# Hybrid decoder block on one core: router weights loaded earlier, into a buffer of their own

## The reference

```python
h = rms_norm(x, g_mix_norm)
proj = h @ w_in                                  # 1024 x 7168: q, k, v, g_ret, u_pool, gate_a, gate_b
merged = sigmoid(gate_a) * (y_ret @ w_branch[0]) + sigmoid(gate_b) * (y_pool @ w_branch[1])
x = x + merged @ w_out
h2 = rms_norm(x, g_ffn_norm)
logits = h2 @ w_router + b_router                # 1024 x 32
top_val, top_idx = top_k(logits, 4); top_w = softmax(top_val)
# every expert e, for the tokens that chose it:
act = swiglu_clamped(h2 @ w_gate_up[e] + b_gate_up[e])     # 1024 x 2048
x += top_w * (act @ w_down[e] + b_down[e])                  # 1024 x 1024
x = x + sigmoid(rms_norm(x, g_ple_norm) @ w_ple_gate) * (p @ w_ple_proj)
y = rms_norm(x, g_final)
```

## Time and profile before

| | before |
|---|---|
| median of three executions | 1283.8 us |
| profiled execution, its time | 1294.33 us |
| profiled execution, its span | 1292.5 us |
| mean granted TensorE clock | 0.957 |
| PE busy | 1219.5 us, 94% |
| DVE, ACT, POOL busy | 383.1, 202.0, 8.3 us |
| bytes moved, share of q1 of the 16 DMA engines | 456.59 MB, 85.2% |
| chain that ended last | PE 74%, DMA 14%, DVE 9% |

### The profile page before, as it was taken

One profiled execution on the slowest core, in us unless ns is written; L12 is line 12 of the kernel. 1 busy time (PEld: TensorE's weight loads), 2 busy tenths in 40 slices (PEclk: granted clock), 3 DMA queues, 4 the chain that ended last, 5 costly groups with the idle time before them and its releaser, 6 DMA issues.

```text
span 1292.5 us, 13525 instructions
## 1 busy us (share of the span) xinstructions
PE 1219.5 (94%) x5404; PEld 612.8 (47%) x5405; DVE 383.1 (30%) x587; ACT 202.0 (16%) x266; POOL 8.3 (1%) x19
## 2 busy tenths in 40 slices
PE   7999999969999999999999899999999999899987
PEld 6888888834443434343434344334344343434335
DVE  6955666521221303030312212202212030303036
ACT  5354444320100000010100000000000000001024
POOL 0000000000000000000000000000000000000000
PEclk9999999979999999999999999899999999999998
DMA  9754355866899999999999999869999999999970
GB/s 363 265 177 163 119 203 188 323 243 277 327 404 423 430 426 417 425 425 421 426 414 417 430 412 427 352 283 426 427 415 428 418 430 407 407 418 429 428 281 33
DMA packets 56621, 456.59 MB, mean 353 GB/s; under 512 B 5406, under 2 KB 6860, under 8 KB 30316
## 3 DMA queue, kind: packets, MB, share of 16 engines
q1 hardware_dynamic: 54320, 451.99, 85.2%
q10 hardware_dynamic: 2268, 4.14, 0.9%
HBM read 455.07 MB, written 1.05 MB: 353 GB/s over the span
## 4 chain that ended last, share of the span: by engine, by line
PE 74%; DMA 14%; DVE 9%; issue 1%; ACT 1%; SPq 0%; DVEq 0%; POOLq 0%; POOL 0%; ACTq 0%
PE ps L559 74%; DMA ring<-in_w_gate_up 12%; DMA B<-in_b_router 2%; DVE B L1469 2%; DVE x L1480 2%; DVE B L1460 2%; DVE B L1465 2%; DVE B L1461 2%; PE ps L566 1%; SPq L475 0%; DMA x<-in_x 0%; DVE over_xn L1257 0%; ACT B L1128 0%; ACT over_hT L1010 0%; PE ps L825 0%
## 5 line engine op out<-in xcount | busy, mean ns | idle before, releaser
L559 PE MATMUL ps<-ring,B 128*64 128x512 f32 x3024 | 685.5, 613 | 14.2 <-DMA ring<-in_w_gate_up 12.7
L559 PEld LDWEIGHTS ps<-ring,B 128*64 128x64 f32 x3024 | 223.7, 141 | 463.6 <-issue 459.8
L1460 DVE TENSOR_SCALAR B<-ps 128x1024 f32<-128x1024 f32 x16 | 19.6, 1225 | 667.5 <-PE ps L559 667.5
L559 PE MATMUL ps<-w_split,over_hT 128*128 128x512 f32 x544 | 173.8, 396 | 2.9 <-DVE w_split L1248 2.7
L1248 DVE TENSOR_TENSOR w_split<-ring,w_split 128x1024 fp32r<-128x1024 f32 x88 | 105.9, 1223 | 72.2 <-ACT w_split L1002 70.3
L559 PEld LDWEIGHTS ps<-w_split,over_hT 128*128 128x128 f32 x544 | 103.0, 191 | 24.7 <-issue 3.1
L559 PE MATMUL ps<-w_split,over_xn 128*128 128x512 f32 x288 | 113.1, 393 | 0.0
L1002 ACT CAST w_split<-ring 128x1024 fp32r<-128x1024 f32 x88 | 91.2, 1054 | 105.3 <-PE ps L559 105.0
L1119 ACT ACTIVATE B<-B 128x1024 f32<-128x1024 f32 x16 | 16.9, 1056 | 570.4 <-DVE B L1460 570.4
L559 PE MATMUL ps<-B 128*128 128x512 f32 (+3 forms) x288 | 92.0, 493 | 1.9 <-ACT B L1128 1.2
L559 PE MATMUL ps<-B,xn 128*128 128x128 f32 x512 | 73.9, 311 | 13.3 <-DVE x L1480 13.3
(11 more groups left out here) (140 smaller groups left out, 384.4 us busy)
## 6 DMA issues: line engine op xcount, KB each, us to landing
ring<-in_w_gate_up SPq DMA_DIRECT2D x120, 2048.0 KB, 13.5
ring<-in_w_down SPq DMA_DIRECT2D x60, 2048.0 KB, 15.9
ring<-in_w_in SPq DMA_DIRECT2D x28, 1024.0 KB, 5.1
ring<-in_w_gate_up SPq DMA_DIRECT2D x12, 1024.0 KB, 9.7
ring<-in_w_branch SPq DMA_DIRECT2D x8, 1024.0 KB, 7.0
ring<-in_w_down SPq DMA_DIRECT2D x6, 1024.0 KB, 13.2
ring<-in_w_out SPq DMA_DIRECT2D x4, 1024.0 KB, 4.9
ring<-in_w_ple_gate SPq DMA_DIRECT2D x4, 1024.0 KB, 16.3
```

Source lines behind the costliest of these rows:

```text
L559: return pe.matmul(out, lhsT, rhs, start=start, stop=stop, skip_group_check=True)
L1460: step(ve.tensor_scalar(gate, two_banks(0), LIMIT, None, ALU.min), s.gate_ready)
```

## The change

Before, the router's weights and bias were pieces of `B[4]`, loaded when the last merge had been read. Now they have a tensor of their own, `router`, 288 numbers in each partition, and the two loads stand behind the four copies of the pooling's mix, ahead of the loads of `b_down` and `g_final`.

```diff
+        router, = sb("router", [P, (KD + 1) * N_EXPERTS])
...
-        w_router = piece(KD * N_EXPERTS).rearrange("p (k e) -> p k e", k=KD)
-        b_router = piece(N_EXPERTS)
+        w_router = router[:, 0:KD * N_EXPERTS].rearrange("p (k e) -> p k e", k=KD)
+        b_router = router[:, KD * N_EXPERTS:]
...
                 nc.scalar.copy(mixedT[:, 2 * j:2 * j + 2, :], bank_cols(4 + j, 2)).then_inc(mixT_ready, 1)
 
+            e.dma_start(w_router, t["w_router"][0].rearrange("(k p) n -> p k n", p=P)).then_inc(router_loaded, 16)
+            e.dma_start(b_router, t["b_router"].to_broadcast([P, N_EXPERTS])).then_inc(router_loaded, 16)
             e.dma_start(b_down, t["b_down"][0]).then_inc(late_loaded, 16)
             e.dma_start(g_final, t["g_final"].unsqueeze(0).to_broadcast([P, D])).then_inc(late_loaded, 16)
             read_block(11, gates[0], ACT.Sigmoid)
...
             e.wait_ge(branch_read, 4)
-            e.dma_start(w_router, t["w_router"][0].rearrange("(k p) n -> p k n", p=P)).then_inc(router_loaded, 16)
-            e.dma_start(b_router, t["b_router"].to_broadcast([P, N_EXPERTS])).then_inc(router_loaded, 16)
             e.dma_start(p_in, t["p"][0, 0].rearrange("(i p) n -> p i n", p=P)).then_inc(p_loaded, 16)
...
-    nc = bacc.Bacc("TRN2", target_bir_lowering=False, num_devices=1)
+    nc = bacc.Bacc("TRN2", target_bir_lowering=False, num_devices=1, dynamic_dma_scratch_size=1024)
```

## The result

| | before | changed |
|---|---|---|
| median, first comparison | 1283.8 us (5 runs) | 1274.95 us (5 runs) |
| ratio, 95% interval | | 0.9914, 0.9894 to 0.9934 |
| second comparison, other runs | 1288.0 us | 1274.46 us, 0.9911 (0.9885 to 0.9936) |
| third | 1288.0 us | 1275.58 us, 0.9906 (0.9882 to 0.9929) |
| profiled execution, its time / span | 1294.33 / 1292.5 us | 1279.28 / 1277.4 us |

The ratio is an estimate of its own from the executions of both kernels, with its 95% interval; it is not the quotient of the two medians, and the two can differ by some us. By the ratios the change gains 0.9%, which is 11 us; by the medians of the first comparison it gains 8.9. The forecast was 1268.6 us, a gain of 15.2.

The account below looks back on a forecast made before the run. The prediction took PE's 9.86 us wait for the router's bias, with half-clock work behind it, as the bound ahead of nearly weight-bound experts. Gains of 12.2 + 2.6 + 0.4 = 15.2 us gave 1268.6 us, range 1264.5 to 1275.

Parts of the forecast that it names:

- The bound and the rigid shift: PE's 9.86 us wait for the router's bias; removing it moves first gate product and weight stream forward together by 15.2 us.
- Term 1: Last transposes to the end of the router's product: wait gone and product at full clock, 12.2 us gained.
- Term 2: From the router's product to the gather: bias products and ranks take 5.1 instead of 7.74 us, 2.6 us gained.
- Term 3: The gather ahead of the first pair: clock dips as in pair 2, 5.7 instead of 6.10 us, 0.4 us gained.
- clock stays up: Rival, from the router on: without the idle time the clock never falls, 16.9 us gained, 1266.9 us; chance 0.18.
- clock is lower for longer: Rival, router to gather: little-work products keep the clock down, 9.5 to 13 us gained, 1271 to 1274.3 us; chance 0.13.
- held at the new place: Rival: the queue takes small descriptors only as they move, holding ACT at about 155 us; slower, 1310 us; chance 0.04.
- swallowed by weights: Rival, experts' stage: PE, 15 us early, waits 15 us for weights; no gain, 1283.8 us; chance 0.05.

Follow-up runs that it names:

- place_only: Changed kernel with its own router tensor and smaller descriptor space, but the router's two loads issued at the old place: 1289.08 us, ratio 1.0019.
- after_fill: Changed kernel with 11 filling products of 128 x 512 on PE ahead of the router's product: 1284.29 us, ratio 0.9973.
- after_again: Changed kernel run again with no edit, against the kernel before: 1274.46 us, ratio 0.9911.
- before_again: Kernel before, unchanged, timed against itself: 1285.85 against 1288.0 us, ratio 0.9988.
- after_third: Changed kernel run once more with no edit, against the kernel before: 1275.58 us, ratio 0.9906.
- fill_wait: Kernel before, loads at the old place, with 11 filling products keeping PE busy during the router wait: 1283.82 us, ratio 0.9976.
- long_rows: Kernel before, loads at the old place, w_router read as 8 whole rows per partition, leaving token routing wrong: 1273.68 us, ratio 0.9869.
- bias_rows_first: Changed kernel with the first pair's bias products over 128 rows instead of 2: 1271.94 us, ratio 0.9861; repeated, 1272.96 us, 0.988.
- bias_rows_all: Changed kernel with the bias products of all 16 pairs over 128 rows instead of 2: 1271.37 us, ratio 0.9852.

## Why the prediction was right, and where its sizes were off

**The bound and the rigid shift: right.** PE waited 9.86 us for a load of 16 KB, and nothing but the time of its issue had to change (place_only). SP's first load behind `used` moved by the same 13.56 us as the first gate product, and 9.6 us of filling cost 8.0 to 9.8 (after_fill against after_again). In eight of the profiles the time from the first gate product to the end is

| loads late | us | loads early | us |
|---|---|---|---|
| before | 995.9 | changed kernel | 994.4 |
| before_again | 993.2 | after_again | 987.9 |
| place_only | 990.1 | after_third | 989.9 |
| fill_wait | 990.6 | after_fill | 990.5 |

The means are 992.5 and 990.7, so early loads don't make this stage longer, as far as eight profiles that scatter over 8 us can tell. The other four profiles lie in the same band: long_rows 989.9, bias_rows_first 989.7 and 994.1, bias_rows_all 992.2.

**Term 1, 12.2 us: right.** The product ended at 281.88 and now ends at 266.33 + 3.64 = 269.97; with the 0.29 us that this execution lags, 12.2. The start right behind the transposes, the 3.5 us (3.64) and DVE's scaling in time all came as worked out. The split into wait and clock is shown by fill_wait.

**Term 2, 2.6 us: measured 2.2.** From the router's end to the gather it is 5.51 us instead of 7.74. The ranks came 4.2 instead of 4.0 after the router's end, and the fourth bias bank ran partly at half clock.

**Term 3, +0.4 us: measured -0.6. This is the step that was mis-sized.** I took from pair 2 that the clock falls 4.8 us after the bias begins and is back 3.4 later. Here it fell after 3.9 and stayed down for about 6.8, so the gather took 6.67 instead of the forecast 5.7; the profiles of after_again, fill_wait, after_fill and long_rows have it down for 6.8 us too. The direction of the weighing was right: products over 2 rows, not idle time, bring the clock down before the gather, so the rival "clock stays up" fell, and bias_rows_first shows both halves of that. What failed is the reason for the size, "the same kind of work in the same order". More pairs would not have helped, since 19 of the 21 stretches at half clock that the kernel before has between 300 and 1250 us last the same 3.4 us. But in pair 2 the bias is followed by gate products over 512 columns, and here by the ranks, the fourth bank and a gather over 128. PE's timeline of the kernel before behind the bias of pair 2:

```profile
405.74 2.59 PE L559 MATMUL ps<-ring,B 128*64 128x512 f32 x8
```

The row for this very place stood in the earlier trace rows: before the change, the clock was down from 284.0 to 294.2, 10.2 us, through the same products. The 6.8 us lie between that and pair 2's 3.4. Why the dip is 6.8 us long stays open: no run varies what stands behind the bias products.

Together 12.2 + 2.2 - 0.6 = 13.8 us, and less the 0.3 lag the 13.56 by which the first gate product moved. It lies between the forecast's 15.2 and the up to 13 of the rival "clock is lower for longer". In its mechanism this rival was half right: the clock was low for twice as long as forecast, though it stayed at 1.00 through the router's product, from 266 to 274.

**From 13.8 to the measured 11.** The three ratios give 11.0, 11.5 and 12.1 us, the medians 8.9, 13.5 and 12.4. The experts' stage alone scatters over 8 us between the profiles above. The upper ends of the gains' intervals are 13.6, 14.8 and 15.2 us, so two of the three hold 13.8, and the first just misses it. The 8.9 owes most to the kernel before, whose median was 1283.8 in that comparison and 1288.0 in the two others, while the changed kernel's stayed within 1.1 us. So the 2.8 us between 13.8 and 11, twice as much as the 1.4 by which the terms were off, are in part scatter. What remains open is whether 1 to 2 us are lost systematically, behind the first gate product or by the new place; no profile shows where. The 15.1 us between the two first spans looked like a full hit and was none: 1.5 us of it is a shorter experts' stage.

**The other rivals.** ACT was not held at the new place: the loads were through in 4 us, and the four issues took ACT 2.87. The gain was not swallowed by weights: the first load behind `used` came at 286.73, where 285 was forecast, and no gate product of the first pair waited for a unit. The landing was far quicker than the 28 us I allowed for, which changed nothing.

## What to carry to other kernels

Here a small load, issued beside a saturated stream, landed late by its number of packets and not by its bytes. Two remedies are to issue it earlier or to give it long rows; either was worth about 1% here, though a version with long rows and the right routing was not run. When a wait of TensorE goes, count also what ran at half clock behind it, but look for other causes of a low clock in the same place before crediting it. How long such a stretch lasts is not safely taken from another place: it was 3.4 us in most pairs, 10.2 at this place before the change and 6.8 after it. Where the next stage is bound by transfers, ask whether those transfers are released by the engine that comes earlier: here they were, and the shift arrived at the end, in full or nearly so.

## What the runs showed of the hardware

- On this kernel, products with 2 of 128 rows are followed by half the TensorE clock although the engine is busy; the same products with 128 rows, 126 of them against zeros, keep it at 2.4 GHz ahead of the first pair (gather 6.62 to 6.78 us in three profiles of the changed kernel, 4.01 in three with 128 rows).
- `p`, behind the router's loads in ACT's queue, landed 29.9 us after issue before, 10.4 in the changed kernel, and 17.4 in long_rows, where fewer packets stood ahead of it: its landing follows the packets ahead of it in its queue.
- A DMA's issue on ACT can take longer when more issues stand before it: 0.44 us for `g_final` behind one other before, 1.43 behind three. Why is open.
- The lowest times of versions that route the tokens as the reference does: the changed kernel with the first pair's bias over 128 rows, 1271.94 and 1272.96 us, and with that of all pairs, 1271.37, which is no different within the scatter.
